# A back-edge hint on TensorE's loop over expert pairs, in a one-core kernel of two transformer blocks

## The reference, cut to what matters

```python
def hierarchical_moe(xn, w_rg, b_rg, w_re, b_re, w1, w3, w2):
    """Top-1 expert group, then top-2 experts inside it; experts are SwiGLU MLPs.
    ...
    """
    ...
    def block_ffn(args):
        tok, e = args
        xb = xt[tok]
        hb = jax.nn.silu(xb @ w1[e]) * (xb @ w3[e])
        return hb @ w2[e]
    ...
    y = jnp.einsum('nk,nkd->nd', gate.astype(xt.dtype), y_assign)
    return y.reshape(B, S, D)
```

## Time and profile before

| what | value |
|---|---|
| median of 3 runs | 1486.57 us (1486.37 to 1487.47) |
| profiled execution, its own time | 1487.96 us |
| its span (first to last instruction) | 1486.2 us |
| TensorE matmuls (PE) | 1373.0 us busy, 92% of the span, 6896 instructions |
| TensorE weight loads (PEld) | 873.2 us, 59%, 6896 instructions |
| VectorE (DVE) | 619.6 us, 42% |
| ScalarE (ACT) | 382.3 us, 26% |
| GpSimd (POOL) | 28.9 us, 2% |
| DMA | 359.64 MB, mean 242 GB/s |
| chain that ended last | PE 71%, DMA 16%, DVE 7%, ACT 3%, issue 3% |

### The profile page before, as it was taken

How to read it: one execution, slowest core, us unless ns; L and a number is a source line. 1 busy time by engine, 2 the same in 40 slices (tenths; PEclk the granted TensorE clock), 3 DMA queues, 4 the chain that set the end, 5 groups by cost and what they waited for, 6 DMA issues and landing times.

```text
span 1486.2 us, 17723 instructions
## 1 busy us (share of the span) xinstructions
PE 1373.0 (92%) x6896; PEld 873.2 (59%) x6896; DVE 619.6 (42%) x1122; ACT 382.3 (26%) x589; POOL 28.9 (2%) x61
## 2 busy tenths in 40 slices
PE   5999997999998999999999999689998887899997
PEld 5978875955645445444444544259744443899843
DVE  4685567433343132232223222236754544544211
ACT  5456564311111111111111111314201231344200
POOL 2000102000000000000000000000000000000000
PEclk9999998999998999999999999899999999899999
DMA  9443539839644799999999999904404144265500
GB/s 343 170 170 137 188 126 333 284 124 339 233 153 183 292 430 429 429 427 429 429 428 429 429 429 427 371 0 142 170 2 183 58 128 153 75 195 186 198 15 14
DMA packets 99819, 359.64 MB, mean 242 GB/s; under 512 B 3906, under 2 KB 29766, under 8 KB 87409
## 3 DMA queue, kind: packets, MB, share of 16 engines
q1 hardware_dynamic: 96640, 349.77, 60.6%
q0 software_dynamic: 3120, 9.05, 2.0%
HBM read 357.76 MB, written 1.05 MB: 241 GB/s over the span
## 4 chain that ended last, share of the span: by engine, by line
PE 71%; DMA 16%; DVE 7%; ACT 3%; issue 3%; SPq 0%; DVEq 0%; ACTq 0%
PE bank L435 26%; DMA ring<-in_w 14%; PE bank L473 11%; PE bank L780 9%; PE bank L991 5%; PE bank L798 3%; PE bank L756 2%; PE bank L482 2%; DMA ring<-in_w_xkv 1%; PE bank L718 1%; PE bank L883 1%; PE bank L893 1%; DVE ring_parts L1024 1%; PE bank L811 1%; PE bank L954 1%
## 5 line engine op out<-in xcount | busy, mean ns | idle before, releaser
L435 PE MATMUL bank<-arena_parts,ring_parts 128*128 128x256 f32 x1920 | 239.5, 289 | 16.8 <-DVE ring_parts L1024 10.8
L435 PEld LDWEIGHTS bank<-arena_parts,ring_parts 128*128 128x128 f32 x1920 | 238.6, 198 | 17.7 <-issue 17.6
L1024 DVE TENSOR_TENSOR ring_parts<-ring,ring_parts 128x1024 fp32r<-128x1024 f32 x148 | 178.5, 1223 | 159.2 <-ACT ring_parts L1672 146.1
L780 PE MATMUL bank<-ring,arena 128*64 128x512 f32 x512 | 226.0, 594 | 10.0 <-DMA ring<-in_w 8.4
L781 PE MATMUL bank<-ring,arena 128*64 128x512 f32 x512 | 226.4, 595 | 0.0
L1672 ACT ACTIVATE ring_parts<-ring 128x1024 fp32r<-128x1024 f32 x148 | 154.4, 1057 | 211.4 <-PE bank L435 210.0
L435 PE MATMUL bank<-ring_parts,arena_parts 128*128 128x512 f32 x816 | 191.3, 395 | 10.1 <-DVE ring_parts L1024 6.4
L435 PEld LDWEIGHTS bank<-ring_parts,arena_parts 128*128 128x128 f32 x816 | 154.4, 191 | 44.7 <-issue 8.1
L473 PE MATMUL bank<-ring,arena 128*128 128x512 f32 x320 | 143.4, 607 | 14.4 <-issue 9.9
L780 PEld LDWEIGHTS bank<-ring,arena 128*64 128x64 f32 x512 | 67.8, 137 | 150.5 <-issue 150.5
L473 PEld LDWEIGHTS bank<-ring,arena 128*128 128x128 f32 x320 | 61.4, 195 | 91.3 <-issue 86.1
(11 more groups left out here) (356 smaller groups left out, 1183.4 us busy)
## 6 DMA issues: line engine op xcount, KB each, us to landing
ring<-in_w SPq DMA_DIRECT2D x96, 2048.0 KB, 16.8
ring<-in_w_in SPq DMA_DIRECT2D x26, 2048.0 KB, 9.1
ring<-in_w_ada SPq DMA_DIRECT2D x12, 2048.0 KB, 8.0
ring<-in_w_ffn_gate SPq DMA_DIRECT2D x11, 1024.0 KB, 5.4
ring<-in_w_ffn_up SPq DMA_DIRECT2D x11, 1024.0 KB, 8.0
ring<-in_w_ffn_down SPq DMA_DIRECT2D x5, 2048.0 KB, 7.8
ring<-in_w_xkv SPq DMA_DIRECT2D x4, 2048.0 KB, 23.0
ring<-in_w_out SPq DMA_DIRECT2D x4, 2048.0 KB, 13.4
```

What stands on the lines that cost most here:

```text
L435: mm = pe.matmul(ps[:, o:o + width], *pair, start=(o == 0 and k == 0 and ha + hw == 0), stop=(k == KD - 1 and ha == 1), skip_group_check=True)
L780: pe.matmul(PS[2][0:C, :], xgT[:, k, j, :], w1u[:, k, :], start=(k == 0), stop=(k == KD - 1))
L1024: dve.tensor_tensor(low, src, high, ALU.subtract).then_inc(low_ready, 1)
```

## The change

```diff
-        def pass_program(eng, settle, step, alone):
+        def pass_program(eng, settle, step, alone, **loop):
 
 
             step(0, 0, False, True)
-            with eng.Fori(1, PAIRS - 1) as i:
+            with nc.Fori(1, PAIRS - 1, engines=[eng.engine], **loop) as i:
                 step(i, 2 * i, True, True)
             step(PAIRS - 1, NE - 2, True, False)
...
             gather(0, 0)
             gather(0, 1)
-            pass_program(pe, settle, step, alone)
+            pass_program(pe, settle, step, alone, hint_back_edge=True)
```

## The result

The change made the kernel slower, by a little: 1490.53 us against 1486.45 us (medians of 7 runs each; 1488.82 to 1493.32 against 1485.81 to 1487.47). The ratio is 1.003, 95% interval 1.0019 to 1.0042, so 4.1 us in the medians. The forecast on record was 1486.6 us and no difference, in a range that ended at 1490.0.

The account below looks back on a forecast made before the run. The prediction took the DMA stream of weights to bound the loop, 29.36 us for each pair. All terms were 0 on the path, so 1486.57 + 0 = 1486.6 us, range 1485.2 to 1490.0 us.

Parts of the forecast that it names:

- The bound of the loop: In the loop, the stream of weights takes 29.36 us for each pair, TensorE's work 28.2; later trips wait for loads.
- the 50 ns taken: Hint at the top of each trip: nearest row 50 ns, 14 times 0.7 us, covered, so 0 on the path.
- the rival I had named as the main way to be slower: Loop's DMA stream: the hint refetches resident code, 1499.2 or 1511.8 us at the high price, 1488.3 at the low; chance 0.09.
- Leaving the loop: At the loop's exit, last branch not taken against the hint: 0, or 0 to about 2 us if code is refetched.
- late code: Behind the loop, code fetched anew: up to 2 us, 6.3 if neither cover holds; chance 0.02 for over 3 us.
- the body is fetched once and stays: In the loop: no instruction packet between 531 and 905 us, the last one before it in the first trip.
- The first cover: Behind the loop, the last pair's wait for weights until 939.01 us was to hide a code fetch of 6.3 us.
- The second cover: At the back edge, TensorE's issuing part is 4.3 us ahead of the array; taken off the 6.3 us fetch at the exit.
- The bound I had written beside it: Behind the loop, late code costs 6.3 us if neither cover holds, up to 1492.9 us.
- The Trainium skill's rule: At the back edge, by this rule each would pay what L339 pays, 6305 ns, and the hint would remove it.

Follow-up runs that it names:

- the two versions without a gap: Against the kernel before: an empty instruction in the hint's place, ratio 1.0003; the loop written out with the hint ahead of `down`, ratio 0.9993.

## Why the prediction was wrong

**What held.** The bound of the loop: the nine waits for loads add up to 8.3 us against 8.4, and the loop takes 405.2 us against 405.6. The back edge cost nothing before and costs nothing now; a hint takes 31 ns, under the 50 ns taken, and is hidden. No resident block was fetched again: no packet on q8 in the whole loop, so the rival I had named as the main way to be slower (0.09) didn't happen. L339 stayed at 6252 ns. The back-edge gaps are the loads', not the branch's.

**What failed** is the step "Leaving the loop", costed at 0, with 0 to about 2 us as its bound and 0.02 for over 3. So the forecast missed by its mechanism, not by a size: a packet that I had taken for the body's own no longer came, and the code behind the loop was late. It costs 3.6 to 4.2 us in the traces compared like with like, and 0.19 to 0.32% of the time (2.8 to 4.8 us) in three comparisons. The sign that I had named for late code, a gap behind "issue" near 923 us, is what the profile shows, at 920.8. Three errors are in the step.

1. I read the earlier trace rows as "the body is fetched once and stays", and didn't ask which block the packet of the first trip was. It came when the body was about to be wholly resident, so it was the block behind it. A hint that redirects a fetch takes a fetch from somebody, and this was the only one in the loop to take. The hint at three places shows it: where the packet stays away the gap is there, and where it comes there is none.

2. The first cover, the last pair's wait for its weights until 939.01 us, is no slack. TensorE's own work reaches `down` at about the same time: L798 started at 939.22 us in the kernel before. With the stall it started at 942.99 us, 5.4 us behind its last load:

```profile
L798 PE MATMUL bank<-ring,arena 128*64 128x512 f32 x64 | 14.2, 595 | 1.1 <-DVE arena L1433 1.1
```

   The 1.1 us ahead of it, which the earlier trace rows put down to the load, are put down to VectorE's L1433 now that the load is long there, and are as long as before. (That load lands at 937.6 us in this trace, 1.4 us earlier than in the trace of the kernel before, as the loop's exit is 1.5 us earlier.)

3. The second cover, the lead of 4.3 us, was measured at the loop's branch and doesn't last. Right behind the branch the issuing part stops at the wait for the pair's weights, for 4.7 us in either kernel (L327 at the loop's exit, the longer of two waits, of the changed kernel):

```profile
L327 PEldq EVENT_SEMAPHORE  x2: 51/2382/4712, 913.2 to 913.3; - x2
```

   It starts again from nothing, and the edge comes 28 instructions later. The cover was 11 matmuls, 920.80 - 918.04 = 2.8 us, out of 6.1. The versions with the edge at 12 and at 188 instructions show how it scales: 5.0 us of gap and none.

The clock added to it in some executions. The stretch behind the gap ran at half clock in the changed kernel's profile; in that of the experiment with the hint behind the first `up` it didn't, and there the stretch from exit to L473 was a microsecond shorter. As the two versions without a gap have a slow stretch of their own, I don't count the clock as a cost of the hint.

The bound I had written beside it, 6.3 us if neither cover holds, was of the right size; only its chance was far too low. The Trainium skill's rule, which I weighed against the back edge (Runtime: NRT & Kernel Launch, "Instruction fetch mechanics": a taken branch out of the window stalls for a page), was rightly found not to bear on it. It bears on L339, with 6.3 us measured, and the stall behind the loop is the same miss without a branch. Its other sentence, that prefetch is purely sequential, doesn't hold where a hint stands: the packet of the sequential block stays away.

## What to carry to other kernels

A branch hint doesn't add a fetch, it redirects one (the whole span has 41 packets on q8 before and after, and 40 with the hint on the skipping branch): before placing it, find in the instruction packets which block is fetched in that stretch now, and who needs it next. Put hints on branches that the trace shows to miss (here the one of 6305 ns, not those of 208 ns), executed well ahead of them, and not on a loop whose whole body is resident. And when an engine's lead is to cover a stall, measure the lead at the place of the stall: a wait for data in between sets it to nothing.

## What the runs showed of the hardware that I had not expected

TensorE kept a loop of 323 instructions through 13 back edges without one instruction packet, and no packet of the next block came for as long as a hint stood at the crossing, through all 14 trips. A missing block cost 6.1 to 6.5 us from the last wait to the resumption, and 6.2 to 6.3 us at a branch, with the DMA queues full. The block that the hint had kept away was fetched 8.7 to 9.0 us behind the loop's exit, whether its edge was 12, 28 or 188 instructions off. A gap of 3.3 us was followed in one trace by some 3 us at a granted clock of 0.51, and in another, after 3.7 us, by none; two traces without the gap had a slower stretch some 20 us later. And where a block's edge happens to lie was worth 6 to 7 us here: moving code by less than one block made a branch of 6305 ns one of 438.
